# Latent attention of the second layer: logits in four PSUM banks, the maximum one unit earlier than the normalisation, and one mask product for two heads

## The reference

```python
def block(args):
    qn, qp, n = args
    s = (jnp.einsum('bihd,bjhd->bhij', qn, k_nope, preferred_element_type=jnp.float32)
         + jnp.einsum('bihd,bjd->bhij', qp, k_pe, preferred_element_type=jnp.float32)) * scale
    qpos = n * Q_BLOCK + jnp.arange(Q_BLOCK)
    s = jnp.where(qpos[:, None] >= kpos[None, :], s, NEG_INF)
    return jnp.einsum('bhij,bjhd->bihd', jax.nn.softmax(s, axis=-1), v)
```

## Time and profile before

| | before |
|---|---|
| median of 3 runs | 1659.46 us |
| lowest and highest | 1658.57 and 1661.36 us |
| profiled execution, its own time | 1660.16 us |
| its span | 1658.4 us |
| PE busy | 1632.7 us, 98% of the span |
| DVE busy | 1180.4 us, 71% |
| ACT busy | 808.8 us, 49% |
| share of the chain that ended last | PE 87%, ACT 5%, DVE 5% |
| latent and last windowed units on PE (unit 8's logits to the projection) | 1416.60 to 1437.61 us |

### The profile page before, as it was taken

One profiled execution on the slowest core, in us unless ns is written; L12 is line 12 of the kernel. 1 busy time (PEld: TensorE's weight loads), 2 busy tenths in 40 slices (PEclk: granted clock), 3 DMA queues, 4 the chain that ended last, 5 costly groups with the idle time before them and its releaser, 6 DMA issues.

```text
span 1658.4 us, 30179 instructions
## 1 busy us (share of the span) xinstructions
PE 1632.7 (98%) x12366; PEld 1547.8 (93%) x12366; DVE 1180.4 (71%) x1636; ACT 808.8 (49%) x1063; POOL 218.1 (13%) x190
## 2 busy tenths in 40 slices
PE   9999999999999999999999999999999999999998
PEld 9999998999999999998999999898988889799887
DVE  6555587795566855577787655787888679788874
ACT  5334374663344534456574344665534446653433
POOL 1001510400033000421030024141000010000000
PEclk9999999999999999999999999999999999999999
DMA  6455453444454445544346655333455533245553
GB/s 234 168 188 200 155 183 137 142 164 177 177 196 148 168 173 185 199 150 169 127 156 214 219 201 183 114 141 128 165 190 196 209 141 124 70 175 179 197 182 127
DMA packets 39153, 279.99 MB, mean 169 GB/s; under 512 B 4880, under 2 KB 6032, under 8 KB 8848
## 3 DMA queue, kind: packets, MB, share of 16 engines
q1 hardware_dynamic: 36896, 270.34, 45.4%
q0 software_dynamic: 2160, 8.29, 1.5%
HBM read 275.10 MB, written 1.05 MB: 167 GB/s over the span
## 4 chain that ended last, share of the span: by engine, by line
PE 87%; ACT 5%; DVE 5%; issue 1%; POOL 1%; DMA 1%; DVEq 0%; SPq 0%; ACTq 0%; POOLq 0%
PE bank L733 21%; PE bank L735 21%; PE bank L734 21%; PE bank L750 8%; PE bank L751 5%; ACT w_hi L1678 2%; DVE w_lo L2389 2%; PE bank L752 1%; ACT h L1738 1%; PE bank L1195 1%; ACT h_both L1737 1%; PE bank L860 1%; PE bank L861 1%; PE bank L866 1%; PE bank L1224 0%
## 5 line engine op out<-in xcount | busy, mean ns | idle before, releaser
L2389 DVE TENSOR_TENSOR w_lo<-raw,w_hi 128x2048 fp32r<-128x2048 f32 (+5 forms) x239 | 562.3, 2354 | 192.5 <-ACT w_hi L1678 192.1
L1678 ACT ACTIVATE w_hi<-raw 128x2048 fp32r<-128x2048 f32 (+5 forms) x247 | 476.1, 1930 | 347.7 <-PE bank L960 122.1
L733 PE MATMUL bank<-h_both,w_hi 128*128 128x272 f32 (+1 forms) x1704 | 490.7, 288 | 2.0 <-DVE w_lo L2389 1.7
L735 PE MATMUL bank<-h_both,w_lo 128*128 128x272 f32 (+1 forms) x1704 | 488.3, 287 | 0.0
L734 PE MATMUL bank<-h_both,w_hi 128*128 128x272 f32 (+1 forms) x1704 | 486.8, 286 | 0.0
L733 PEld LDWEIGHTS bank<-h_both,w_hi 128*128 128x128 f32 x1704 | 321.1, 188 | 5.6 <-DVE w_lo L2389 3.7
L735 PEld LDWEIGHTS bank<-h_both,w_lo 128*128 128x128 f32 x1704 | 321.2, 188 | 0.0
L734 PEld LDWEIGHTS bank<-h_both,w_hi 128*128 128x128 f32 x1704 | 320.8, 188 | 0.1
L733 PE MATMUL bank<-g_both,w_hi 128*128 128x272 f32 (+1 forms) x934 | 269.4, 288 | 0.7 <-DVE w_lo L2389 0.4
L734 PE MATMUL bank<-g_both,w_hi 128*128 128x272 f32 (+1 forms) x934 | 265.9, 285 | 0.0
L735 PE MATMUL bank<-g_both,w_lo 128*128 128x272 f32 (+1 forms) x934 | 265.6, 284 | 0.0
(11 more groups left out here) (437 smaller groups left out, 2521.8 us busy)
## 6 DMA issues: line engine op xcount, KB each, us to landing
raw<-in_up_w SPq DMA_DIRECT2D x111, 1024.0 KB, 4.7
raw<-in_down_w SPq DMA_DIRECT2D x40, 1408.0 KB, 5.8
raw<-in_in_w SPq DMA_DIRECT2D x20, 1024.0 KB, 4.7
raw<-in_up_w SPq DMA_DIRECT2D x16, 1152.0 KB, 5.0
raw<-in_out_w SPq DMA_DIRECT2D x16, 1024.0 KB, 4.8
raw<-in_even_w SPq DMA_DIRECT2D x12, 1024.0 KB, 4.8
raw<-in_last_down SPq DMA_DIRECT2D x11, 1024.0 KB, 4.7
raw<-in_odd_w SPq DMA_DIRECT2D x6, 1024.0 KB, 4.8
```

Source lines behind the costliest of these rows:

```text
L733: pe.matmul(out, w[0], x[0], start=first, stop=False)
L735: return pe.matmul(out, w[1], x[0], start=False, stop=last)
L1678: last = act.activation(into[:, lo:hi], raw[:, slot, lo:hi], ACT.Copy)
L2389: last = dve.tensor_tensor(lo[:, b:n], raw[:, slot, b:n], hi[:, b:n].bitcast(F32), ALU.subtract)
```

## The change

Only the logits, maxima and normalisations of the second group (units 8 to 15) are touched.

```diff
--- before.py
+++ after.py
@@ -535,6 +535,10 @@
         ODD_UNITS = [(p, t, slice(h, h + 3 - p, 2 - p)) for p in range(2) for t in range(2)
                      for h in ((0, 2, 4, 6) if p else (0, 1, 4, 5))]
 
+        def score_bank(u):
+
+            return 4 + u % 2 if u < 10 else (0, 1, 4, 5)[(u - 10) % 4]
+
         def unit_banks(u, start):
 
             return ps[0:4] if u >= start and u % 2 else ps[4:8]
@@ -1512,21 +1516,25 @@
                     if u == 0:
                         pe.wait_ge(c_std, 2)
                 else:
-                    pe.wait_ge(qd_roped, heads.start + 2)
+                    pe.wait_ge(qd_roped, heads.start + 2 if u < 10 else 8)
                     pe.wait_ge(kd_ready, 2)
                     pe.wait_ge(kn_copied, 2)
-                if u >= 2:
-                    pe.wait_ge(od_max if u < 10 else od_exp, u - 1)
+                if 2 <= u < 10:
+                    pe.wait_ge(od_max, u - 1)
+                elif u >= 12:
+                    pe.wait_ge(od_exp, u - 3)
                 for e, hd in enumerate(range(8)[heads]):
-                    out = ps[4 + u % 2][:, e * S:e * S + P * (t + 1)]
+                    out = ps[score_bank(u)][:, e * S:e * S + P * (t + 1)]
                     if p == 0:
                         last = pe.matmul(out, half(qc, hd, t * P, P),
                                          kdup[64 * (hd % 2):64 * (hd % 2) + 64, hd // 4, 0:P * (t + 1)], start=True, stop=True)
                     else:
                         pe.matmul(out, qd[:, hd, t * P:(t + 1) * P], kd[:, hd, 0:P * (t + 1)],
-                                  start=True, stop=False)
-                        last = pe.matmul(ps[4 + u % 2][:, e * S + t * P:e * S + (t + 1) * P], ident_r[:],
-                                         mask_r[:, t, :], start=False, stop=True)
+                                  start=not e, stop=False)
+                if p:
+                    own = ps[score_bank(u)][:, :].rearrange("p (e n) -> p e n", e=2)[:, :, t * P:(t + 1) * P]
+                    mask = mask_r[:, t, :].rearrange("p (a n) -> p a n", a=1).broadcast_to([P, 2, P])
+                    last = pe.matmul(own, ident_r[:], mask, start=False, stop=True)
                 last.then_inc(od_s, 1)
 
             def transposes(u):
@@ -2278,7 +2286,7 @@
                 if u >= 2:
                     act.wait_ge(od_t, u - 1)
                 for e, hd in enumerate(range(8)[heads]):
-                    src = ps[4 + u % 2][:, e * S:e * S + P * (t + 1)] if p else att_s[:, u % 2, e, 0:1 + P * (t + 1)]
+                    src = ps[score_bank(u)][:, e * S:e * S + P * (t + 1)] if p else att_s[:, u % 2, e, 0:1 + P * (t + 1)]
                     col = slice(hd, hd + 1)
                     last = act.activation(att_p[:, u % 2, e, p:1 + P * (t + 1)], src, ACT.Exp,
                                           bias=o_max[:, 2 * p + t, col], accum_out=o_sum[:, 2 * p + t, col])
@@ -3314,7 +3322,7 @@
 
                 p, t, heads = ODD_UNITS[u]
                 b, keys, out = u % 2, P * (t + 1), o_max[:, 2 * p + t, heads]
-                bank = ps[4 + b]
+                bank = ps[score_bank(u)]
                 dve.wait_ge(od_s, u + 1)
                 if p:
                     dve.tensor_reduce(out, bank[:, :].rearrange("p (e n) -> p e n", e=2)[:, :, 0:keys], AX.X, ALU.max,
@@ -3418,8 +3426,10 @@
                     rotated(2 * u - 8)
                     rotated(2 * u - 7)
                 largest(u)
-                if u > 4:
+                if u < 9:
                     normalised(u - 1)
+                elif u > 9:
+                    normalised(u - 2)
                 if u == 8:
                     split_next(2 * KD, 0, 3, False, 0)
                 elif u == 9:
@@ -3427,6 +3437,7 @@
                     split_next(2 * KD, 0, 3, False, 1)
                 elif u == 12:
                     low_part(0, 1)
+            normalised(14)
             normalised(15)
             low_part(1, 0)
             low_part(1, 1)
```

## The result

The changed kernel takes 1673.31 us in the median of 4 runs (1672.08 to 1676.20); the kernel before, on the same chips, 1659.70 (4 runs, 1658.57 to 1661.36). The ratio of the executions is 1.0088 with a 95% interval of 1.0077 to 1.0100 (the two medians by themselves give 1.0082): 0.9% slower. 1670.3 was predicted, with a range of 1666.5 to 1677.0.

A forecast was written before the change was run, and what follows sets the result against it. PE was taken to bound the kernel (87% of the last chain). 9.1 us of serial waits plus 1.7 for one clock fall made 10.8 on 1660.16, so 1671.0, less 0.7 for the median: 1670.3; range 1666.5 to 1677.

The forecast's parts named there:

- the series: Attention stage: transposes of u - 2 wait for normalisation behind the maximum of just-written logits u; 9.1 us lost.
- the wait before unit 8's transposes: PE idle 2.6 to 2.9 us, as unit 8's normalisation stands behind both low halves and unit 10's maximum.
- the waits before those of units 9 to 13: PE idle before each of these transposes, released by DVE's normalised weights; 1.1 to 1.5 us each.
- a step: Units 12 and 13, from logits to the next logits: 3.25 us in place of 1.83.
- 9.1 us: Attention stage: total lost to the serial order, mask saving included; 8.5 to 9.7 by the mask's unknown price.
- the mask product: PE's logits: one product for two heads instead of two, taken to save 0.12 us a unit (0 to 0.24).
- one such fall: Behind unit 8's long wait, PE's clock halves for 3.4 us; cost 1.7 us.
- the forecast's case: Whole kernel: serial loss plus one fall of the clock, 1670.3 us; chance 0.45.
- the second rival: From unit 8's transposes on, low clock for much of the stage: about 1675 us, 1679.6 at worst; chance 0.26.
- 1668.6: Whole kernel in us if the serial loss comes with no fall of the clock; chance 0.22.
- Faster: Attention stage: DVE normalises u - 2 before PE reaches its transposes, saving 2.0 us, so 1657.5; chance 0.03.
- Won back later: Behind the stage: transfers going on during the delay return more than 6 us, to within 0.2%; chance 0.03.

The follow-up runs named there:

- the clock held up: Changed kernel with 70 useless PE products filling the waits before the transposes of units 8 to 13; 1668.63 us, ratio 1.0054 to the kernel before.
- PE ahead: Changed kernel with PE also writing logits of unit u + 1 before the transposes of u - 2, from step 9 on; 1663.72 us, ratio 1.0032.

## Why the prediction was right, and where its size was off

**Right: the series.** "Logits, maximum, normalisation and transposes are now in series in each step" is what the timelines show, and undoing DVE's order alone takes away all of the loss, adding it alone brings all of it. Item by item at full clock: the wait before unit 8's transposes was to be 2.6 to 2.9 us and was 2.96; the waits before those of units 9 to 13 were to be 1.1 to 1.5 and were 1.11 to 1.51; a step was to be 3.25 and was 3.36. In the sum, 9.1 us were worked out for the stage and 9.68 measured with the clock held up. The difference is two small terms: transposes and weighted values, taken from rows without a wait in front (0.69, where they take 0.74 behind one), and the mask product, whose worth was put at 0.12 and measures 0.06.

**Too small: the clock.** "I count one such fall: +1.7" was the step that failed. The profiled execution had six times the length of one fall, 20.4 us at 1.2 GHz, and that cost 16.3 - 9.7 = 6.6 us in the stage; the median over the runs puts it at 13.6 - 9.7 = 3.9 us. The profiled execution is the slowest of the four: their mean granted clocks are 0.990, 0.991, 0.993 and 0.994, where the kernel before has 0.996 or 0.997, so by an estimate from these figures the others spent from about 8 to 18 us more at half the clock than the kernel before. The median lies between the forecast's case and the second rival's ("low clock for much of the stage"), the profiled execution in the rival's. (Half of the rival's 11 us on top of 1668.6 is 1674.1, where the prediction has about 1675.) The ground given against that rival, "no row shows such waits lowering the clock", was true of the rows and no reason: the trace before holds no run of repeated waits of that kind. Nor did the ground for counting exactly one fall, a wait longer than the mean of 2.3 us, say what it seemed to: of the four waits in that mean, those of 2.18, 2.09 and 2.18 us (ending at 1158.92, 1350.09 and 1464.31) had a fall behind them, and the longest, 2.89 us (ending at 1035.69), had none. The profiled executions with filled waits show both that the low clock ended after one fall where PE was kept busy behind it, and that waits of 1.2 to 1.6 us in each step can bring the clock down by themselves. What the Trainium skill tells of a kernel in which every burst begins at the half clock (TensorE: Matmul & The Clock Gate, "HAM oscillation — how this bites in real kernels") was nearer to the truth here than I let it be, with the clock at 0.50 through three steps of the profiled execution, though not to the letter: in the version with the delay one unit later the series of waits passed with the clock at 1.00.

**What a low clock costs.** The prediction let 3.4 us at the half clock cost half of it, 1.7; in the kernel with only the later waits filled, one fall cost 1.26 us of the stage. In the profiled execution of the changed kernel 20.4 us cost 6.6, a third. The wait for DVE in a step stays the same (1.38 us at full clock, 1.37 or 1.38 at half), and the rest of a step takes 3.52 us at half in place of 1.98, which is 1.8 times and not twice.

**The rivals.** *Faster* needed DVE to be done before PE came to the transposes; it comes nearly true only with PE ahead. With DVE's delay one unit later that gave the time of the kernel before (ratio 0.9999); with DVE's old order the medians are 1.5 and 1.8 us lower, which is not beyond their intervals. *Won back later* did not happen: the two profiled executions differ by 16.0 us and their stages by 16.3. The range held because it reached to the low clock, and not because the one fall was right.

## What to carry to other kernels

When one engine is told to work one unit ahead, write down for every pair of engines which step each wait hangs on: a producer that asks for the result of unit u - 2 right after it has written unit u, while the engine between them takes unit u first, gains nothing from more buffers, and the pipeline becomes a series. Price such a series twice, once for the waits and once for the clock that PE may lose in them, and do not take the price of one long wait for that of many short ones. Delay a normalisation only where the producer of the logits has moved as well; in this kernel it gained nothing even then.

## What the runs showed of the hardware that I had not expected

- Extra products can make a program faster: 70 products without use, in time that PE would have waited, took it from 1673.31 to 1668.63 us, and the granted clock stayed at 1.00 in the stage.
- Waits of at most 1.6 us, one in each step, were followed by a fall of the clock in one profiled execution and by none in another. The four waits for ACT of 2.1 to 2.9 us elsewhere in the kernel (9.3 us together) were followed by three falls in the profiled execution of the kernel before and by none in that of the version with the delay one unit later: the same waits do not always bring the same falls.
- A product of 256 columns against two of 128: 0.06 us less for each unit, with a mask operand repeated by a broadcast and no sign that the repetition costs anything.
